# A hybrid decoder trunk on one core: one semaphore wait and three row loads moved, the LRU convolution cut in chunks, its gate products in fp32r passes

## The chip, the core and the metric

One of the cores of a Trainium2 chip runs the whole kernel. The metric is the device time of one execution in microseconds (us), as the median of several runs; lower is better. Five engines work side by side, each through its own list of instructions in the order in which it was written: TensorE (PE in the rows, its weight loads PEld), VectorE (DVE), ScalarE (ACT), GpSimd (POOL) and SyncE (SP), which here only issues DMAs. They meet through semaphores: an instruction may wait until a counter has a value, and an engine stands still while its next instruction waits.

## The reference, cut to what matters

Four layers, each `x + W_out(mixer(RMSNorm(x)) * silu(gate))`, over 1024 prompt positions and 8 sample positions, in fp32. The mixers are retention (layers 0 and 3), differential attention (layer 1) and the RG-LRU block (layer 2). What the change touches of it:

```
def retention_chunk(S0, qkv, lg):                        # layers 0, 3: 4 heads, 8 chunks of 128
    o = einsum('bihd,bhdv->bihv', q, S0) * q_dec + (q k^T * decay) v
    S = exp(C * lg) * S0 + einsum('bjhd,bjhv->bhdv', k * k_dec, v)
...
def rg_lru_branch(h, ...):                               # layer 2: 12 blocks of 128 channels
    xb, g = split(h @ w_in, 2)
    xconv = conv_b + sum(xc[:, kk:kk + T] * conv_w[kk] for kk in range(4))   # per channel, 4 taps
    r = sigmoid(einsum('btnc,ncd->btnd', xblk, wa) + ba)                     # the gate products,
    i = sigmoid(einsum('btnc,ncd->btnd', xblk, wx) + bx)                     # 128x128 per block
    a = exp(-8 * r * softplus(-lam)); b = sqrt(1 - a^2) * (i * xconv)
    hs = scan(h <- a h + b);  out = (hs * silu(g)) @ w_out
```

## The kernel before

**Tiling.** Activations lie with channels on the 128 partitions and the T = 1032 positions along a row; a row of `xT` is one tile of 128 channels. The positions are cut in `CHUNKS` of 384, 384 and 264 columns (`NC_` = 3). A *unit* is 128 output channels: for each chunk, eight 128x128 weight tiles times the chunk. Every projection keeps fp32 precision by splitting weight and input in a high and a low part of type fp32r and making three passes for each tile: high x high (L301), low input (L302), low weight (L303). A chunk of a unit is thus 24 matmuls.

**Weights.** SP loads a unit's weights (`load_w`, L240, 512 KB); ACT rounds them to the high part (`split_hi`, L248, two halves of 512 columns); POOL subtracts for the low part (`split_lo`, L257, two halves); PE takes them from there.

**Order.** Nothing is scheduled by a program: each engine's list is written out by hand, one function for each stage and engine (`ret_pe`, `lru_act`, `out_sp`, ...).

**Retention (layers 0, 3).** For each head, after its projections, PE walks eight chunks r. A step transposes (L944), then adds up the output in the bank OB: three matmuls of the scores with the values (L953 to L955) and, for r > 0, two matmuls of the queries with the state (L959); then come the products for the state update (L964, L965). DVE adds them to the state (L1159, L1160) and counts semaphore `r_su`. PE waits for `r_su` of the step before, with two other semaphores, ahead of L953.

**Output stage of layers 0 and 3.** SP (`out_sp`, L717 to L754) loads `w_out` units and, four DMAs a chunk (`stage_load`, L414), the mixer's output and gate from HBM into a buffer that holds two chunks; chunk 2 goes into the place of chunk 0 and so waits for `h_raw`. DVE multiplies them (`stage_dve`, L435), ACT and DVE split the product (L334, L341), PE multiplies, DVE adds to `xT` (`residual_dve`, L445). Six rows of `xT` (`AWAY_ROWS`) were in HBM while their space held other data. `x_reload` (L757 to L759) brings one back (128x1032, 516 KB); each row has its own semaphore in `x_back`, and the first residual of a row waits for it.

**LRU (layer 2).** Twelve blocks. A block has six chunks s on PE: s = 0 to 2 are the block's `xb`, s = 3 to 5 its `g`. ACT copies s = 0 to 2 from PSUM into `xpad` (L1964). DVE then copies the block's parameters `lp` (L2033), three small pieces (L2038 to L2040), and runs the convolution `xcv` over the whole row: tap by tap, a small instruction for the 8 sample positions and one over 1024 columns (L2045 to L2050). PE's gate products (L1931: two weights `wax` times three chunks of `xcv`, as six fp32 matmuls; twelve records in the trace) stand between s = 4 and s = 5 and wait for the whole convolution (`l_xc`). On ACT, `split_hi` of the next unit's weights, the tanh of g (`g_tanh`, L1953) and the tanh of the gates (L1981) follow; DVE multiplies by g (`g_mul`, L2060) and scans (L2085); POOL makes the product with g (L2112) once the scan is done, and SP stores it (L1872) and issues the next weight loads behind that store.

Of the kernel before, what the change touches and what calls it, by code (L numbers as in the profile page):

```python
# [145 lines left out]
def trunk(nc, A, LAYERS=4):  # L146
    ctx = ExitStack()
    with ctx:
# [64 lines left out]
        x_saved, x_back = sem("x_saved"), sems("x_back", KT)  # L213
# [224 lines left out]
        def residual_dve(dve, unit, q, j, c, final, sqb, sqn, back):  # L438
# [4 lines left out]
            if back is not None and c == 0 and j < AWAY_ROWS:  # L443
                dve.wait_ge(x_back[j], back)
# [183 lines left out]
        def ret_sp(sp, lay):  # L628
# [59 lines left out]
            head(RH - 1)  # L688
            out_sp(sp, lay, wout, U + 48, R + 48, [(FILL_AT[lay] + 1, 0), (FILL_AT[lay] + 2, KT)], ret_stage_wait,
# [175 lines left out]
        def out_dve(dve, ch, lay, U, fills, last_layer, scale, beside=None, begun=False):  # L865
# [4 lines left out]
            for x, (f, k0) in enumerate(fills):  # L870
# [10 lines left out]
                for q, (j, c) in enumerate(out_order(more or final)):  # L881
                    residual_dve(dve, unit, q, j, c, final, sqb, sqn, 16 * (lay // 3 + 1) if lay in (0, 3) and x == 0 else None)
# [36 lines left out]
        def ret_pe(pe, lay):  # L919
            f = FILL_AT[lay]  # L920
            def head(h, first):
                unit, raw, n1, n8, ntr = ret_places(lay, h)
                for s in range(36):
# [22 lines left out]
                    if 0 <= t - 1 < NBLK:  # L946
# [905 lines left out]
        tmp_s = al.take(NS)  # L1852

        l_ld, l_set, l_z = sem("l_ld"), sem("l_set"), sem("l_z")
        l_xc = sem("l_xc")
# [7 lines left out]
        CREDITS += [(x, 1) for x in (l_xc, l_tg, l_at, l_m, l_sq, l_h, l_th, l_pr)] + [(l_gt, 12)]  # L1863
# [53 lines left out]
        def lru_pe(pe):  # L1917
            def block(n, slot, pair, first=False):
                unit, n1, n2, n3, n6 = lru_at(n)
                for s in range(6):  # L1920
                    if not (first and s < NC_):
                        unit_chunk(pe, unit, s // NC_, s % NC_, LF)
                    if s == 4:
                        pe.wait_ge(l_set, 1)
                        pe.wait_ge(l_xc, done(n1.at(0)))
                        pe.wait_ge(l_wl[slot], pair * 32 + 32)
# [7 lines left out]
            block(0, 0, 0, True)  # L1934
            block(1, 1, 0)
            for i in range(1, LRU_B // 2):
                block(i * 2, 0, i)
                block(i * 2 + 1, 1, i)
# [300 lines left out]
```

## Time and profile before

| what | value |
|---|---|
| median of 3 runs | 3273.43 us (3272.81 to 3280.8) |
| the profiled execution, its own time | 3276.99 us |
| its span in the profile | 3275.2 us |
| PE busy | 3120.3 us (95%), 19978 matmuls |
| DVE, ACT, POOL busy | 1372.2 us (42%), 1267.7 us (39%), 561.9 us (17%) |
| projection passes L301, L302, L303 busy | 1633.6, 1574.7, 1574.0 us |
| gate products L1931 busy | 33.1 us (384 columns) and 12.7 us (264 columns) |
| DMA | 459.78 MB, mean 140 GB/s |

The profile's busy time of PE overlaps (matmuls are pipelined, their ends are modelled), so what PE really loses is read from the distance between starts in the timeline: two 384-column matmuls start about 0.175 us apart, and every longer distance is a wait. "[0.58 <-DVE arena L1160]" behind a row says that the engine stood idle for 0.58 us before it and that the end of DVE's L1160 released it. "x4" joins instructions of one line that follow each other.

### The profile page before, as it was taken

How to read it: one execution, taken by the hardware profiler on the slowest of the kernel's cores; microseconds unless marked ns; L12 is line 12 of the kernel's file. 1: busy time of each engine (PE TensorE's matmuls, PEld its weight loads, DVE VectorE, ACT ScalarE, POOL GpSimd, SP SyncE). 2: the span in 40 equal slices, each digit the busy share in tenths (PEclk: the TensorE clock that was granted, in tenths of full speed). 3: DMA queues.
4: the chain of work that ended last, by engine and by line, in shares of the span. 5: the costliest groups of instructions: out<-in, count | busy, mean ns of one | idle time of the engine just before them, and what ended most of it. 6: DMA issues, size and time to landing. Idle time of an engine off the chain costs nothing.

```text
span 3275.2 us, 51546 instructions
## 1 busy us (share of the span) xinstructions
PE 3120.3 (95%) x19978; PEld 2838.0 (87%) x19978; DVE 1372.2 (42%) x3480; ACT 1267.7 (39%) x2709; POOL 561.9 (17%) x432
## 2 busy tenths in 40 slices
PE   6999999998998999999979899989799999999899
PEld 4989898997997888888859899979798989899799
DVE  3241514226344444444445777763524151422631
ACT  4332423334234555455543455532433332333321
POOL 1112021111211111011101223222111211111121
PEclk8999999999999999999999999999999999999999
DMA  5848586776413444444453122232234242425742
GB/s 164 256 151 248 168 245 194 213 240 224 145 56 116 139 136 155 142 147 143 141 187 100 34 64 63 64 106 82 63 125 129 88 148 89 151 78 163 240 138 80
DMA packets 531892, 459.78 MB, mean 140 GB/s; under 512 B 25091, under 2 KB 464387, under 8 KB 531651
## 3 DMA queue, kind: packets, MB, share of 16 engines
q1 hardware_dynamic: 425570, 334.75, 32.8%
q10 hardware_dynamic: 106080, 121.74, 10.8%
q8 instruction: 160, 2.62, 0.3%
q14 instruction: 82, 0.66, 0.1%
HBM read 354.39 MB, written 169.14 MB: 160 GB/s over the span
## 4 chain that ended last, share of the span: by engine, by line
PE 79%; DVE 10%; issue 4%; ACT 4%; DMA 2%; ACTq 1%; SPq 1%; POOL 0%; DVEq 0%
PE psum L301 20%; PE psum L302 20%; PE psum L303 20%; PE psum L959 3%; PE psum L1419 2%; DVE Hl L341 2%; PE psum L1392 2%; DVE hraw L385 2%; PE psum L936 1%; DVE hraw L435 1%; PE psum L1408 1%; PE psum L1931 1%; PE psum L1462 1%; PE psum L976 1%; PE psum L1431 1%
## 5 line engine op out<-in xcount | busy, mean ns | idle before, releaser
L301 PE MATMUL psum<-Hh,Wh 128*128 128x384 f32 (+1 forms) x4896 | 1633.6, 334 | 92.9 <-DVE Hl L341 31.6
L302 PE MATMUL psum<-Hl,Wh 128*128 128x384 f32 (+1 forms) x4896 | 1574.7, 322 | 0.0
L303 PE MATMUL psum<-Hh,Wl 128*128 128x384 f32 (+1 forms) x4896 | 1574.0, 321 | 0.0
L301 PEld LDWEIGHTS psum<-Hh,Wh 128*128 128x128 f32 x4896 | 931.5, 190 | 147.7 <-issue 55.0
L257 POOL TENSOR_TENSOR Wl<-wraw,Wh 128x512 fp32r<-128x512 f32 (+1 forms) x416 | 533.3, 1303 | 2518.3 <-ACT Wh L248 2517.2
L302 PEld LDWEIGHTS psum<-Hl,Wh 128*128 128x128 f32 x4896 | 932.3, 190 | 6.2 <-issue 0.3
L303 PEld LDWEIGHTS psum<-Hh,Wl 128*128 128x128 f32 x4896 | 930.2, 190 | 0.0
L248 ACT ACTIVATE Wh<-wraw 128x512 fp32r<-128x512 f32 (+1 forms) x416 | 235.1, 615 | 267.3 <-PE psum L303 148.2
L445 DVE TENSOR_TENSOR xT<-psum,xT 128x384 f32<-128x384 f32 x168 | 86.3, 514 | 294.8 <-PE psum L303 294.1
L334 ACT ACTIVATE Hh<-hraw 128x384 fp32r<-128x384 f32 (+1 forms) x252 | 116.5, 489 | 153.8 <-DVE hraw L435 82.4
L1020 ACT ACTIVATE hraw<-psum 128x384 f32<-128x384 f32 (+1 forms) x96 | 44.0, 458 | 279.3 <-PE psum L303 279.3
L1166 DVE SCALAR_TENSOR_TENSOR arena<-arena 128x512 f32<-128x512 f32 x128 | 98.4, 820 | 106.5 <-ACT arena L1069 106.5
L1128 DVE TENSOR_TENSOR vtl<-psum,vth 128x384 fp32r<-128x384 f32 (+1 forms) x96 | 48.6, 506 | 212.0 <-ACT vth L1042 212.0
L1660 ACT ACTIVATE arena<-arena 128x256 f32<-128x256 f32 (+7 forms) x128 | 98.2, 769 | 86.7 <-DVE arena L1725 86.7
L341 DVE TENSOR_TENSOR Hl<-hraw,Hh 128x384 fp32r<-128x384 f32 (+1 forms) x252 | 119.5, 510 | 13.7 <-ACT Hh L334 13.2
L1122 DVE SCALAR_TENSOR_TENSOR ktl<-psum,arena,kth 128x384 fp32r<-128x384 f32 (+1 forms) x48 | 27.5, 573 | 216.8 <-ACT kth L1039 216.8
L1721 DVE CUSTOM_DVE_ANT_0 arena<-psum,arena 128x256 f32<-128x256 f32 (+7 forms) x128 | 91.9, 754 | 47.0 <-PE psum L1392 45.5
L1026 ACT ACTIVATE arena<-psum 128x384 f32<-128x384 f32 (+1 forms) x96 | 44.0, 458 | 166.7 <-PE psum L303 166.7
L959 PE MATMUL psum<-arena 128*128 128x512 f32 x224 | 105.2, 592 | 0.0
L600 DVE TENSOR_SCALAR arena<-arena 128x1 f32<-128x1 f32 x72 | 11.1, 154 | 208.7 <-ACT hraw L1064 208.7
L1074 ACT ACTIVATE arena<-psum,arena 128x512 f32<-128x512 f32 x64 | 44.1, 689 | 117.0 <-DVE arena L607 117.0
L456 ACT ACTIVATE arena<-xT 128x384 f32<-128x384 f32 (+1 forms) x72 | 35.4, 491 | 132.2 <-DVE xT L445 132.2
(212 smaller groups left out, 3164.7 us busy)
## 6 DMA issues: line engine op xcount, KB each, us to landing
wraw<-in_ret_w_in SPq DMA_DIRECT2D x96, 512.0 KB, 4.4
scratch_kc<-in_cache_kt SPq DMA_DIRECT2D x64, 512.0 KB, 6.4
scratch_vc<-in_cache_vt SPq DMA_DIRECT2D x64, 512.0 KB, 6.7
arena<-in_state_ret ACTq DMA_DIRECT2D x64, 512.0 KB, 6.9
out_ret_state_sample<-arena ACTq DMA_DIRECT2D x64, 512.0 KB, 5.1
arena<-scratch_kc SPq DMA_DIRECT2D x64, 512.0 KB, 4.3
arena<-scratch_vc SPq DMA_DIRECT2D x64, 512.0 KB, 4.5
scratch_on<-arena ACTq DMA_DIRECT2D x78, 256.0 KB, 2.4
```

What stands on the lines that cost most here:

```text
L248: act.activation(Wh[:, j % 2, x], wraw[:, j % 2, x], ACT.Copy).then_inc(w_hi, 1)
L257: pool.tensor_tensor(Wl[:, j % 2, x], wraw[:, j % 2, x], Wh[:, j % 2, x].bitcast(F32), ALU.subtract)\
L301: nc.tensor.matmul(out, hi, xh, start=(k == 0), stop=False)
L302: nc.tensor.matmul(out, hi, xl, start=False, stop=False)
L303: last = nc.tensor.matmul(out, lo, xh, start=False, stop=(k == kt - 1))
L334: act.activation(Hh[:, k, c0:c0 + w], hraw[:, n % HR, 0:w], ACT.Copy).then_inc(h_hi, 1)
L341: nc.vector.tensor_tensor(Hl[:, k, c0:c0 + w], hraw[:, n % HR, 0:w], Hh[:, k, c0:c0 + w].bitcast(F32), ALU.subtract).then_inc(h_lo, 1)
L445: nc.vector.tensor_tensor(xT[:, j, c0:c0 + w], bank[q % 2][:, 0:w], xT[:, j, c0:c0 + w], ALU.add)\
L959: last = nc.tensor.matmul(OB[:, :], qdT[:, r % 2, x, :], St[:, x, :], start=False, stop=(x == 1))
L1166: last = nc.vector.scalar_tensor_tensor(sring[:, b % 4, x, :], vbr[:, b % 4, :], kT[:, x, SEQ + b:SEQ + b + 1], sring[:, b % 4, x, :], ALU ...
L1660: act.activation(x, x, ACT.Exp, bias=nm2[:, s % 2, m:m + 1], accum_out=(l8[:, s:s + 1], l1[:, s % 2:s % 2 + 1])[m]).then_inc(d_ex, 1)
L1721: nc.vector.tensor_tensor_reduce(out=(S0[t % 3], S1[t % 2])[m][:, 0:W], in0=SSC[m][:, 0:W], in1=strip[:, SEQ - W:SEQ], scale=1.0, scalar=- ...
```

## The change

Four edits, all in the hand-written orders.

1. **Row reloads.** Three of the six rows of `xT` are issued at the end of the last retention head, each behind a value of `r_st`, ahead of the first `w_out` load; the others go one place earlier in `out_sp`. Rows share a semaphore in pairs, and a residual waits for both rows of its pair (32).
2. **State wait.** PE's wait for `r_su` stands behind the three score matmuls, ahead of L960.
3. **Convolution by chunk.** DVE runs the four taps chunk by chunk (`conv(0)`, `conv(1)`, `conv(2)`) and makes a low part of each chunk (`conv_low`, into `xcl`) from a high part that ACT rounds (`conv_high`, into `xch`). ACT also rounds the gate weights (`wxh`), POOL subtracts for `wxl` (`gate_lo`, between the two units' `split_lo`).
4. **Gate products.** Eighteen fp32r matmuls (three passes, two weights, three chunks) take the place of six fp32 ones, still between s = 4 and s = 5; each chunk waits for its own `l_xl`.

```
-                        pe.wait_ge(r_su, prior(n8.at(r)))
                         nc.tensor.matmul(OB[:, :], sdh[:, r % 2, :], vth[:, r, :], start=True, stop=False)
...
                         last = nc.tensor.matmul(OB[:, :], sdl[:, r % 2, :], vth[:, r, :], start=False, stop=(r == 0))
+                        pe.wait_ge(r_su, prior(n8.at(r)))
...
             head(RH - 1)
+            for k in range(3):
+                sp.wait_ge(r_st, done(8 * RH * (j_ + 1) - 8 + 2 * k + 2))
+                x_reload(sp, lay, k)
...
-                        if lay in (0, 3):
-                            x_reload(sp, lay, j)
...
-                    if lay in (0, 3) and x == 0 and j < AWAY_ROWS:
-                        x_reload(sp, lay, j)
+                    if lay in (0, 3) and x == 0 and j + 1 < AWAY_ROWS:
+                        x_reload(sp, lay, j + 1)
...
-                                nc.tensor.matmul(bank[2 + 3 * x + c][:, 0:w], wax[:, slot, x, :], xcv[:, c0:c0 + w],
-                                                 start=True, stop=True).then_inc(l_gt, 1)
+                            pe.wait_ge(l_xl, done(n3.at(c)))
...
+                                nc.tensor.matmul(out, wxh[:, x, :], xch[:, c0:c0 + w], start=True, stop=False)
+                                nc.tensor.matmul(out, wxh[:, x, :], xcl[:, c0:c0 + w], start=False, stop=False)
+                                nc.tensor.matmul(out, wxl[:, x, :], xch[:, c0:c0 + w], start=False, stop=True)\
+                                    .then_inc(l_gt, 1)
...
+                act.wait_ge(l_wl[n % 2], n // 2 * 32 + 32)
+                act.activation(wxh, wax[:, n % 2, :, :], ACT.Copy).then_inc(l_wh, 1)
...
                 split_hi(act, unit, unit, 2)
+                def conv_high(c):
+                    act.wait_ge(l_xc, done(n3.at(c)))
+                    act.activation(xch[:, c0:c0 + w], xcv[:, c0:c0 + w], ACT.Copy).then_inc(l_xh, 1)
+                conv_high(0)
+                conv_high(1)
                 g_tanh(0)
+                conv_high(2)
                 g_tanh(1)
...
+                def conv_low(c):
+                    dve.wait_ge(l_xh, done(n3.at(c)))
+                    nc.vector.tensor_tensor(xcl[:, c0:c0 + w], xcv[:, c0:c0 + w], xch[:, c0:c0 + w].bitcast(F32),
+                                            ALU.subtract).then_inc(l_xl, 1)
+                conv(0)
+                conv(1)
+                conv_low(0)
+                conv(2)
                 nc.vector.tensor_copy(lo[:, OC:OC + 3], xpad[:, SEQ:SEQ + 3])
...
+                conv_low(1)
                 g_mul(0)
+                conv_low(2)
                 g_mul(1)
```

PE, one step of the retention, r > 0, before:

```order
L944 MATMUL psum<-ident,arena 128x128 x3
L953 MATMUL psum<-vth,sdh 128x512 [waits r_su,r_on,r_sd]
L954 MATMUL psum<-vtl,sdh 128x512
L955 MATMUL psum<-vth,sdl 128x512
L959 MATMUL psum<-arena 128x512 [waits r_qd]
```

and with the change:

```order
L945 MATMUL psum<-ident,arena 128x128 x3
L953 MATMUL psum<-vth,sdh 128x512 [waits r_on,r_sd]
L954 MATMUL psum<-vtl,sdh 128x512
L955 MATMUL psum<-vth,sdl 128x512
L960 MATMUL psum<-arena 128x512 [waits r_qd,r_su]
```

Three matmuls now stand ahead of the wait for the state.

SP at the end of layer 0, from the first `w_out` load to the loads of chunk 2, before (`xT<-in_x_cols` is a row reload, `arena<-scratch_on` and `arena<-scratch_g` are the chunk loads; 128x4x264 is chunk 2):

```order
L240 DMA wraw<-in_ret_w_out 128x8x128 [waits raw_free]
L414 DMA arena<-scratch_on 128x4x384 [waits r_g_st0,r_on_st0,r_on_st1,r_qz,r_g_st1,r_qd,r_os_st,r_sn,r_st]
...
L759 DMA xT<-in_x_cols 128x1032
L240 DMA wraw<-in_ret_w_out 128x8x128 [waits raw_free]
L414 DMA arena<-scratch_on 128x4x384 [waits r_so,r_S_st,r_su,r_o]
...
L759 DMA xT<-in_x_cols 128x1032 x2
L240 DMA wraw<-in_ret_w_out 128x8x128 [waits raw_free]
L759 DMA xT<-in_x_cols 128x1032
L414 DMA arena<-scratch_on 128x4x264 [waits h_raw]
```

and with the change:

```order
L760 DMA xT<-in_x_cols 128x1032 [waits r_st] x3
L240 DMA wraw<-in_ret_w_out 128x8x128 [waits raw_free]
L414 DMA arena<-scratch_on 128x4x384 [waits r_g_st0,r_on_st0,r_on_st1,r_qz,r_g_st1,r_qd,r_os_st,r_sn,r_st]
...
L240 DMA wraw<-in_ret_w_out 128x8x128 [waits raw_free]
L414 DMA arena<-scratch_on 128x4x384 [waits r_so,r_S_st,r_su,r_o]
...
L760 DMA xT<-in_x_cols 128x1032
L240 DMA wraw<-in_ret_w_out 128x8x128 [waits raw_free]
L760 DMA xT<-in_x_cols 128x1032
L414 DMA arena<-scratch_on 128x4x264 [waits h_raw]
```

Between the first load of chunk 0 and that of chunk 2 there were four row reloads, and there are two.

DVE in one LRU block, before (L2046 and L2050 are the taps, L2060 is `g_mul`):

```order
L2033 COPY arena<-arena 128x41 [waits dve_own]
L2038 COPY arena<-arena 128x3 [waits l_gt,unit_ev,dve_own]
...
L2046 TENSOR_SCALAR arena<-arena 128x1024
...
L2050 SCALAR_TENSOR_TENSOR arena<-arena 128x1024
...
L2050 SCALAR_TENSOR_TENSOR arena<-arena 128x1024
L2060 SCALAR_TENSOR_TENSOR arena<-arena,psum 128x384 [waits unit_ev,l_th] x2
```

and with the change (L2069 and L2072 are the taps, L2081 is `conv_low`, L2097 is `g_mul`):

```order
L2050 COPY arena<-arena 128x41 [waits dve_own]
L2069 TENSOR_SCALAR arena<-arena 128x384 [waits unit_ev,l_gt,dve_own]
L2072 SCALAR_TENSOR_TENSOR arena<-arena 128x384 [waits dve_own] x3
L2069 TENSOR_SCALAR arena<-arena 128x384 [waits unit_ev]
L2072 SCALAR_TENSOR_TENSOR arena<-arena 128x384 [waits dve_own] x3
L2081 TENSOR_TENSOR xcl<-arena,xch 128x384 [waits l_xh]
L2065 TENSOR_SCALAR arena<-arena 128x8 [waits unit_ev]
...
L2072 SCALAR_TENSOR_TENSOR arena<-arena 128x256
L2088 COPY arena<-arena 128x3
...
L2081 TENSOR_TENSOR xcl<-arena,xch 128x384 [waits l_xh]
L2097 SCALAR_TENSOR_TENSOR arena<-arena,psum 128x384 [waits unit_ev,l_th]
```

The first low part, which waits for ACT, now stands ahead of the last chunk's taps.

ACT in the same block, before (L1964 copies into `xpad`, L248 rounds the next unit's weights, L1953 is `g_tanh`, L1981 the gates):

```order
L1964 ACTIVATE arena<-psum 128x256
L248 ACTIVATE Wh<-wraw 128x512 [waits unit_ps,w_loaded0]
L248 ACTIVATE Wh<-wraw 128x512
L1953 ACT_TABLE_LOAD [waits l_pr]
L1953 ACTIVATE arena<-psum 128x384 [waits unit_ps]
L1953 ACTIVATE arena<-psum 128x384 [waits l_pr,unit_ps]
L1981 ACTIVATE arena<-psum,arena 128x384 [waits l_gt] x4
```

and with the change (L1978 is `conv_high`):

```order
L1972 ACTIVATE arena<-psum 128x256
L248 ACTIVATE Wh<-wraw 128x512 [waits unit_ps,w_loaded0]
L248 ACTIVATE Wh<-wraw 128x512
L1978 ACTIVATE xch<-arena 128x384 [waits l_xc] x2
L1959 ACT_TABLE_LOAD [waits l_pr]
L1959 ACTIVATE arena<-psum 128x384 [waits unit_ps]
L1978 ACTIVATE xch<-arena 128x264 [waits l_xc]
L1959 ACTIVATE arena<-psum 128x384 [waits l_pr,unit_ps]
L1998 ACTIVATE arena<-psum,arena 128x384 [waits l_gt] x4
```

Both high parts that PE needs first stand behind a wait for the weight load `w_loaded0`.

## Rows read from the trace of the kernel before

**Rows 1.** Page, busy time, share and instructions of each engine.

```profile
PE 3120.3 (95%) x19978; PEld 2838.0 (87%) x19978; DVE 1372.2 (42%) x3480; ACT 1267.7 (39%) x2709; POOL 561.9 (17%) x432
```

**Rows 2.** PE timeline, two retention steps: start, us, engine, line, operation [idle <-releaser].

```profile
191.76 0.60 PE L944 MATMUL psum<-ident,arena 128*128 128x128 f32 x4
192.95 0.47 PE L953 MATMUL psum<-vth,sdh 128*128 128x512 f32 x1 [0.58 <-DVE arena L1160]
...
193.73 1.02 PE L959 MATMUL psum<-arena 128*128 128x512 f32 x2
...
201.50 0.60 PE L944 MATMUL psum<-ident,arena 128*128 128x128 f32 x4
201.86 0.48 PE L953 MATMUL psum<-vth,sdh 128*128 128x512 f32 x1
```

**Rows 3.** What PE's L953 waited for in the whole span: us, times.

```profile
  DVE arena L1160: 13.2, 24
```

**Rows 4.** PE timeline, first matmul of chunk 2 in layers 0 and 3.

```profile
818.00 0.39 PE L301 MATMUL psum<-Hh,Wh 128*128 128x264 f32 x1 [2.73 <-DVE xT L445]
...
3106.11 0.39 PE L301 MATMUL psum<-Hh,Wh 128*128 128x264 f32 x1 [2.82 <-DVE xT L445]
```

**Rows 5.** SP timeline, layer 0: fourth reload, first load of chunk 2.

```profile
798.76 5.04 SPq L759 DMA_DIRECT2D xT<-in_x_cols  x1
803.84 0.43 SPq L414 DMA_DIRECT2D arena<-scratch_on  x1
```

**Rows 6.** DVE timeline, layer 0: first products of chunk 2.

```profile
814.51 1.12 DVE L435 SCALAR_TENSOR_TENSOR hraw<-arena 128x264 f32<-128x264 f32 x3 [3.94 <-DMA arena<-scratch_g]
```

**Rows 7.** Windows: each engine's busy us, granted clock, DMA share, GB/s.

```profile
736.00:746.00 10.00, 9.73 (x59) 8.12 (x57) 5.14 (x19) 4.09 (x8) 0.00 (x0) 1.00 0.15 47
...
816.00:826.00 10.00, 7.88 (x58) 7.67 (x59) 6.10 (x16) 4.36 (x10) 3.21 (x3) 1.00 1.08 365
...
3106.90:3110.30 3.40, 3.40 (x18) 3.40 (x17) 2.46 (x7) 1.06 (x3) 0.00 (x0) 0.51 1.06 375
```

**Rows 8.** PE timeline, gate products of an LRU block; the last row, the next block's.

```profile
1959.22 0.34 PE L303 MATMUL psum<-Hh,Wl 128*128 128x384 f32 x1
1959.40 3.64 PE L1931 MATMUL psum<-arena 128*128 128x384 f32 x12
1962.68 0.48 PE L301 MATMUL psum<-Hh,Wh 128*128 128x264 f32 x1
1963.00 0.28 PE L302 MATMUL psum<-Hl,Wh 128*128 128x264 f32 x1
...
1986.08 0.81 PE L1931 MATMUL psum<-arena 128*128 128x384 f32 x2
```

**Rows 9.** DVE timeline, the same block: parameters, second tap, fourth tap.

```profile
1949.64 1.21 DVE L2033 COPY arena<-arena 128x41 f32<-128x41 f32 x1
...
1953.31 1.28 DVE L2050 SCALAR_TENSOR_TENSOR arena<-arena 128x1024 f32<-128x1024 f32 x1
...
1956.23 2.38 DVE L2050 SCALAR_TENSOR_TENSOR arena<-arena 128x1024 f32<-128x1024 f32 x1
```

**Rows 10.** ACT timeline, the same block.

```profile
1955.52 1.15 ACT L248 ACTIVATE Wh<-wraw 128x512 fp32r<-128x512 f32 x2 [4.08 <-DMA wraw<-in_lru_w_in]
1956.69 1.28 ACT L1953 ACT_TABLE_LOAD   x1
```

**Rows 11.** POOL timeline, the same block: low parts of two units.

```profile
1949.52 2.52 POOL L257 TENSOR_TENSOR Wl<-wraw,Wh 128x512 fp32r<-128x512 f32 x2
1956.23 3.52 POOL L257 TENSOR_TENSOR Wl<-wraw,Wh 128x512 fp32r<-128x512 f32 x2 [4.19 <-ACT Wh L248]
```

**Rows 12.** ACT's waits in 1844 to 2160: us, times, longest.

```profile
ACT Wh L248 <- DMA wraw<-in_lru_w_in: 40.9, 10, 4.4
```

**Rows 13.** PE timeline, last LRU block: gates, then chunk s = 5.

```profile
2154.61 0.55 PE L301 MATMUL psum<-Hh,Wh 128*128 128x264 f32 x1 [4.36 <-DVE arena L2060]
```

**Rows 14.** ACT timeline, last LRU block.

```profile
2150.93 1.15 ACT L248 ACTIVATE Wh<-wraw 128x512 fp32r<-128x512 f32 x2 [12.27 <-DMA wraw<-in_lru_w_out]
```

More of the change, by code:

```diff
@@ L881, in out_dve @@
                 for q, (j, c) in enumerate(out_order(more or final)):
-                    residual_dve(dve, unit, q, j, c, final, sqb, sqn, 16 * (lay // 3 + 1) if lay in (0, 3) and x == 0 else None)
+                    residual_dve(dve, unit, q, j, c, final, sqb, sqn, 32 * (lay // 3 + 1) if lay in (0, 3) and x == 0 else None)
                     sqn += final
@@ L1862, in trunk @@
         l_oev = sem("l_oev")
-        CREDITS += [(x, 1) for x in (l_xc, l_tg, l_at, l_m, l_sq, l_h, l_th, l_pr)] + [(l_gt, 12)]
+        CREDITS += [(x, 1) for x in (l_xc, l_xh, l_xl, l_wh, l_wlo, l_tg, l_at, l_m, l_sq, l_h, l_th, l_pr)] + [(l_gt, 12)]
         CREDITS += [(x, 16) for x in (l_hst,)]
@@ L1917, in lru_pe, with block @@
         def lru_pe(pe):
-            def block(n, slot, pair, first=False):
+            def block(n, first=False):
                 unit, n1, n2, n3, n6 = lru_at(n)
@@ L1924, in block @@
                         pe.wait_ge(l_set, 1)
-                        pe.wait_ge(l_xc, done(n1.at(0)))
-                        pe.wait_ge(l_wl[slot], pair * 32 + 32)
+                        pe.wait_ge(l_wlo, done(n1.at(0)))
                         pe.wait_ge(l_tg, prior(n6.at(0)))
@@ L1929, in block @@
                             c0, w = CHUNKS[c]
+                            pe.wait_ge(l_xl, done(n3.at(c)))
                             for x in range(2):
-                                nc.tensor.matmul(bank[2 + 3 * x + c][:, 0:w], wax[:, slot, x, :], xcv[:, c0:c0 + w],
-                                                 start=True, stop=True).then_inc(l_gt, 1)
[L1934 to L1938, printed above, removed]
+                                out = bank[2 + 3 * x + c][:, 0:w]
+                                nc.tensor.matmul(out, wxh[:, x, :], xch[:, c0:c0 + w], start=True, stop=False)
+                                nc.tensor.matmul(out, wxh[:, x, :], xcl[:, c0:c0 + w], start=False, stop=False)
+                                nc.tensor.matmul(out, wxl[:, x, :], xch[:, c0:c0 + w], start=False, stop=True)\
+                                    .then_inc(l_gt, 1)
+            block(0, True)
+            for n in range(1, LRU_B):
+                block(n)
             out_pe(pe, 2, LU + LRU_IN, [(6, 0), (7, KT)], LAST == 2)
@@ L2037, in block, with conv @@
                 oc = lo[:, OCS:OCS + 24].rearrange("p (b r) -> p b r", r=3)
+                def conv(c):
+                    c0, w = CHUNKS[c]
+                    dve.wait_ge(unit_ev, ev_val(unit.at(0), c))
+                    wp = min(w, SEQ - c0)
+                    for k in range(4):
+                        tap = lp[:, LW + k:LW + k + 1]
+                        src = xpad[:, c0 + k:c0 + k + wp]
+                        if wp < w:
+                            src_s = cs[:, :, k] if k < 3 else xs8
+                            if k == 0:
+                                nc.vector.tensor_scalar(xcv[:, SEQ:T], src_s, tap, lp[:, LB:LB + 1], ALU.mult, ALU.add)
+                            else:
+                                nc.vector.scalar_tensor_tensor(xcv[:, SEQ:T], src_s, tap, xcv[:, SEQ:T], ALU.mult, ALU.add)
+                        if k == 0:
+                            ins = nc.vector.tensor_scalar(xcv[:, c0:c0 + wp], src, tap, lp[:, LB:LB + 1], ALU.mult,
+                                                          ALU.add)
+                        else:
+                            ins = nc.vector.scalar_tensor_tensor(xcv[:, c0:c0 + wp], src, tap, xcv[:, c0:c0 + wp],
+                                                                 ALU.mult, ALU.add)
+                        if k < 3:
+                            ch.link(ins)
+                    ins.then_inc(l_xc, 1)
+                def conv_low(c):
+                    c0, w = CHUNKS[c]
+                    dve.wait_ge(l_xh, done(n3.at(c)))
[5 more added lines that the diff above has]
+                conv(2)
                 nc.vector.tensor_copy(lo[:, OC:OC + 3], xpad[:, SEQ:SEQ + 3])
@@ L2103, in lru_pool, with gate_lo @@
         def lru_pool(pool):
+            def gate_lo(n):
+                pool.wait_ge(l_wh, done(n))
+                pool.tensor_tensor(wxl, wax[:, n % 2, :, :], wxh.bitcast(F32), ALU.subtract).then_inc(l_wlo, 1)
             def block(n, js):
@@ L2106, in block @@
                     split_lo(pool, Pos(LU, n, 2), j + 1)
+                    if j == js[0]:
+                        gate_lo(n)
                 product(n)
@@ L2118, in lru_pool @@
                 split_lo(pool, Pos(LU, LRU_B - 1, 2), j + 1)
+                if j == 0:
+                    gate_lo(LRU_B - 1)
             out_pool(pool, 2, LU + LRU_IN, [(6, 0), (7, KT)], LAST == 2, beside={3: lambda: product(LRU_B - 1)})
```

30 lines of the change are left out of this document (10 added, 20 removed).

## The prediction

> **What bounds the kernel now.** I read the busy table first: PE is busy for 3120.3 of 3275.2 us, the other engines for less than half [rows 1]. So only what changes the distance between starts on PE can move the time, and I looked at PE's timeline at the four places that the change touches: the retention steps, where PE stands idle ahead of L953 until DVE's state update ends [rows 2]; the output stage of layers 0 and 3, where chunk 2 starts late [rows 4]; the gate products of an LRU block, with no idle time ahead of them [rows 8]; and the end of the last LRU block [rows 13]. Then I followed the engine that PE waits for, or will wait for, at each place: SP and DVE in the output stage [rows 5, 6], DVE, ACT and POOL in the LRU block [rows 9 to 12].
>
> The sum is made against the profiled execution, 3276.99 us, which lies 3.56 above the median of the runs, 3273.43; I take that off at the end. About 0.3% (9.8 us) is what a measurement of this kernel can tell from no change, so "faster" is below 3263.6 and "slower" above 3283.3.
>
> **The state wait.** In a stalled step L953 starts 1.19 us after L944, in a free one 0.36 us after it [rows 2]: 0.83 lost. With the wait behind three matmuls, which take 0.78 (192.95 to 193.73 [rows 2]), L953 starts at 192.12, the three are through at 192.90, and the state comes at the same moment as before, so that L960 starts at about 192.95 where L959 started at 193.73: 0.78 won. What triggers DVE's update is PE's own work of the step before, so the chain moves along with PE and the gain stays in each step. There are 24 such waits, 13.2 us of idle time, 0.55 each [rows 3]. That idle time is the low bound of the gain, 24 x 0.78 = 18.7 the high one; I take 24 x 0.69 = 16.5, the middle and a little, since the weight load of L960 can now lie behind the wait as well. **-16.5 (-13.2 to -18.7).** Nothing else is queued behind this wait but PE itself.
>
> **The row loads.** Chunk 2 starts after 2.73 us of idle time in layer 0, 2.82 in layer 3 [rows 4]. The releaser shown is a residual, but that residual stood on DVE behind the products of chunk 2, and these waited 3.94 us for a load that landed at about 814.5 [rows 6], although SP issued the first of them at 803.84 [rows 5]. The reload just ahead of it took 5.04 us to issue, the load itself 0.43 [rows 5]: the queue was full. At 365 GB/s, with a DMA share of 1.08 [rows 7], one row (516 KB, 0.528 MB) takes 1.45 us. Two rows fewer ahead of chunk 2 make it 2.9 us earlier, against 2.73 and 2.82 needed: just enough. If both gaps close that is -5.5, and the half-speed stretch behind the second goes too: 3.40 us at a granted 0.51, the 1.2 GHz level [rows 7], half of which is 1.7. Together -7.2; what DVE still has to do ahead of the residual can keep a part. The three rows now go out during the last head, where the DMA share is 0.15 (736 to 746 [rows 7]), so they cost nothing there; the first w_out load now stands behind them on SP, behind the value of r_st for r = 6, and if it came late, PE would lose that time one for one. **-6 (-7.2 to 0).** Joining two rows to one semaphore makes a residual wait for its neighbour's row too; both are issued long before, so 0.
>
> **The gate products alone.** Now they take 1959.40 to 1962.68, 3.28 us [rows 8]. A 384-column pass starts 0.18 us after the one before (1959.22 to 1959.40 [rows 8]), a 264-column one by its columns 0.12. Twelve and six of them: 12 x 0.175 + 6 x 0.12 = 2.8. The first matmul behind the fp32 products also took 0.32 instead of 0.12 (1962.68 to 1963.00 [rows 8]). Saved: 0.46 to 0.66 a block, if no operand is late.
>
> **Their operands.** PE wants chunk 0 at 1959.40 and chunk 1 at 1959.40 + 6 x 0.175 = 1960.45. I put the new instructions in the time of that block.
>
> ACT: it waits 4.08 us for the weight load, then rounds until 1956.67 [rows 10]; ten blocks wait so, 40.9 us in all [rows 12]. Both high parts are queued behind this. At 0.5 us each (1.15 for two of 512 columns [rows 10]) they end at 1957.2 and 1957.7.
>
> DVE: one tap over 1024 columns takes 1.28 [rows 9], three products of 264 columns 1.12 [rows 6]; for 384 columns that is 0.5, so conv(0) and conv(1) take 2.1 each, conv(2) 2.3 with its small sample taps, a low part 0.54, the three copies about 0.5. The parameters are there at 1950.85 [rows 9].
>
> POOL: two halves take 2.52 when alone [rows 11], the new gate_lo (256 columns) about 0.7. DVE and POOL hold each other up: the fourth tap took 2.38 where the second took 1.28 [rows 9], just while POOL's pair took 3.52 instead of 2.52 [rows 11], and a copy of 41 elements took 1.21 beside POOL's first half of the other pair [rows 9, 11].
>
> Put together: POOL's second half and gate_lo run until about 1952.8 against conv(0); conv(1) ends at about 1956.7. From there DVE has conv_low(0), conv(2), the copies and conv_low(1) before chunk 1 can go: 0.54 + 2.3 + 0.5 + 0.54 = 3.9. With no hindrance, and from 1957.2 when the first high part is there, it ends at 1961.1; PE then waits 0.65. With every half of POOL in the way, in both pairs, it ends at about 1963.35; PE waits 2.9. I take 1962.25, a wait of 1.8, nearer to the second, since the rows show the taking of turns in this very place. Net for a block: -0.46 + 1.8 = +1.35, bounds 0.65 - 0.66 = 0 and 2.9 - 0.46 = +2.45. What hid the convolution until now was PE's chunk s = 4; that cover ends at 1959.40. Blocks 1 to 10: **+13.5 (0 to +24.5).** Block 0 has no such load to wait for: -0.3.
>
> [...]
>
> **The last block.** ACT waits 12.27 us for the w_out load, until 2150.93 [rows 14]; the gates ran during that wait, and PE then stood 4.36 us until g_mul at 2154.61 [rows 13]. Now the gates stand behind the high parts, which stand behind that wait: 2150.93 + 1.15 + 0.5 = 2152.6 for conv_high(0), then DVE's 3.9 gives 2156.5, or 2159.0 with POOL's pair (2.52), then PE's chunks 1 and 2 (1.05 + 0.72): s = 5 at 2158.3 to 2160.8, 3.7 to 6.2 later than 2154.61. **+5.**
>
> **The clock.** After 2.82 us of idle time the granted clock fell to 0.51, after 2.73 it stayed at 1.00 (816 to 826) [rows 4, 7]. A wait of 1.8 lies below both, but comes in each block; I put in +1, for less than one such stretch of 1.7.
>
> Sum: 3276.99 - 16.5 - 6 + 13.5 - 0.3 + 5 + 1 = 3273.7; less 3.56: **3270 us**, no change that can be told.
>
> **The rivals.** (a) *Faster, about 3257.* DVE gets through the conv in time, because POOL's halves fall in its idle moments: the wait is 0.65, LRU blocks give 0. Then 3270 - 13.5 = 3256.5. For it: DVE is idle most of the time [rows 1]. Against it: the place is just where POOL and DVE meet [rows 9, 11]. Chance 0.22. (b) *Slower, about 3289.* DVE's work in line costs PE 2.9 us ahead of gate chunk 1 in blocks 1 to 10, and that is past the 2.82 at which the clock was seen to fall: +11 on the forecast, and 1.7 in half of the blocks is +8.5 more: 3289; in all of them 3297. It decides at an idle time of between 2.73 and 2.82 us. For it: 0.51 after 2.82 [rows 4, 7]; against: 1.00 after 2.73, and the wait may be shorter. Chance 0.15. (c) *The state wait only moves.* Another semaphore ahead of L960, or its weights, keeps PE for the same time: 3270 + 16.5 = 3286. Against it: in the stalled step only the state was late [rows 2]. Chance 0.05. (d) *The row loads do not do what they are for.* Chunk 2 is late because the queue is full with or without the two rows: 3270 + 6 = 3276. The 1.45 us for a row leave only 0.1 to spare, so this can be; chance 0.08.
>
> **How the numbers follow.** My forecast, 3262 to 3280 by itself, has 0.5. Faster by over 0.3%: (a) and 0.06 of the forecast's low end, 0.28. Slower: (b), (c) and a little of the forecast, 0.2. Within 0.3%: 0.52. The range from 3256 to 3288 takes in (a), (c), (d) and the low part of (b).
>
> **What would show it.** L953 without idle time and L960 with under 0.15: the state wait is right. Chunk 2 of the output stages without its 2.7 us: the row loads. In an LRU block, a period between gate products of about 28.0 where it was 26.68 (1959.40 to 1986.08 [rows 8]), with an idle time of 1.8 released by the second conv_low in the middle of the gates: the operands. A period at or below 26.7 gives (a); one above 29, with a clock near 0.5 behind the gates, (b). The forecast is wrong if the retention steps show no gain, or if PE waits in a place that I have not named.

## The result, and the profile after

| | before | changed |
|---|---|---|
| median | 3275.03 us (20 runs) | 3280.06 us (20 runs, 3274.18 to 3286.57) |
| ratio to before | | 1.0014, 95% interval 1.0008 to 1.0021 |
| profiled execution, span | 3275.2 us | 3274.0 us |

By the ratio the change makes the kernel 4.6 us slower (0.14%); the prediction had said 3270, some 3 to 5 us faster than before. The time is inside the range of what was called "no change", but the sign is wrong. The profiled execution of the changed kernel is one of its fastest: its span lies some 4 us under that of its median run. So its parts are read from it, and their sum from the medians. The state wait, the row loads and the gate products by themselves behaved nearly as forecast; the LRU layer as a whole cost more than the first two gave.

**The state wait.** PE timeline after, the step of [rows 2], and behind it what the weight loads of L960 (PEld) waited for in the whole span (us, times, longest):

```profile
188.12 0.60 PE L945 MATMUL psum<-ident,arena 128*128 128x128 f32 x4
188.48 0.48 PE L953 MATMUL psum<-vth,sdh 128*128 128x512 f32 x1
...
189.27 1.06 PE L960 MATMUL psum<-arena 128*128 128x512 f32 x2
```

```profile
PEld psum L960 <- DVE arena L1161: 3.8, 17, 0.4
```

L953 follows L944 (now L945) after 0.36 us, as in a free step, and L960 starts 1.15 us after L945 where L959 had started 1.97 us after L944. The 13.2 us of idle time [rows 3] are gone: no matmul of L960 stands idle for over 0.15 us anywhere in the span. The 3.8 us are idle time of the weight loads, which overlap the matmuls.

**The row loads.** PE timeline after, the two places of [rows 4]:

```profile
804.39 0.39 PE L301 MATMUL psum<-Hh,Wh 128*128 128x264 f32 x1 [0.93 <-DVE xT L445]
```

```profile
3106.05 0.39 PE L301 MATMUL psum<-Hh,Wh 128*128 128x264 f32 x1 [0.85 <-DVE xT L445]
```

2.73 and 2.82 have become 0.93 and 0.85.

**The LRU layer.** What PE waited for in the LRU blocks (1840 to 2180: us, times, longest; ten of the fourteen waits stand ahead of gate chunk 1 in the blocks 1 to 10), and the PE timeline of one block's gates (1949.15), of another's (2010.84):

```profile
PE psum L1937 <- DVE xcl L2081: 28.5, 14, 7.5
```

```profile
1948.68 0.34 PE L303 MATMUL psum<-Hh,Wl 128*128 128x384 f32 x1
1949.15 0.41 PE L1937 MATMUL psum<-xch,wxh 128*128 128x384 f32 x1
...
1950.11 0.33 PE L1939 MATMUL psum<-xch,wxl 128*128 128x384 f32 x1
1952.24 0.45 PE L1937 MATMUL psum<-xch,wxh 128*128 128x384 f32 x1 [1.80 <-DVE xcl L2081]
1952.52 0.33 PE L1938 MATMUL psum<-xcl,wxh 128*128 128x384 f32 x1
```

```profile
2010.84 0.45 PE L1937 MATMUL psum<-xch,wxh 128*128 128x384 f32 x1 [1.80 <-DVE xcl L2081]
...
2012.00 0.42 PE L1937 MATMUL psum<-xch,wxh 128*128 128x264 f32 x1
2012.22 0.42 PE L1938 MATMUL psum<-xcl,wxh 128*128 128x264 f32 x1
```

The wait is there, in its place, and 1.80 us long. In the second block the passes over 264 columns then start 0.22 us apart, where they normally take 0.12: the clock has fallen. The windows after say which blocks: each engine's busy us, the granted clock (third number from the end), DMA share, GB/s.

```profile
1947.00:1975.00 28.00, 25.80 (x160) 24.74 (x159) 23.47 (x37) 14.15 (x25) 7.22 (x6) 1.00 0.21 62
...
2005.00:2034.00 29.00, 27.09 (x161) 26.48 (x161) 24.00 (x37) 15.21 (x27) 8.40 (x7) 0.94 0.20 60
```

Four of the ten blocks that wait read 0.94, the other six 1.00. A mean of 0.94 over 29 us is 3.5 us at half speed, which by itself would lose about 1.7 us (an estimate). A block at full clock has a period of 28.34 (1949.15 to the next block's gates at 1977.49) where [rows 8] have 26.68.

Why the wait is 1.80 is seen on DVE, ACT and POOL in the same block (L2128 and L2050 are the copies, L2069 and L2072 the taps, L2081 `conv_low`):

```profile
1936.82 2.24 DVE L2128 COPY arena<-arena 128x36 f32<-128x36 f32 x1
1939.09 1.22 DVE L2050 COPY arena<-arena 128x41 f32<-128x41 f32 x1
1940.35 1.38 DVE L2069 TENSOR_SCALAR arena<-arena 128x384 f32<-128x384 f32 x1
1941.76 2.38 DVE L2072 SCALAR_TENSOR_TENSOR arena<-arena 128x384 f32<-128x384 f32 x3
1944.06 0.47 DVE L2069 TENSOR_SCALAR arena<-arena 128x384 f32<-128x384 f32 x1
1944.57 2.87 DVE L2072 SCALAR_TENSOR_TENSOR arena<-arena 128x384 f32<-128x384 f32 x3
1947.36 1.64 DVE L2081 TENSOR_TENSOR xcl<-arena,xch 128x384 fp32r<-128x384 f32 x1
...
1951.63 0.55 DVE L2081 TENSOR_TENSOR xcl<-arena,xch 128x384 fp32r<-128x384 f32 x1
```

```profile
1945.02 1.15 ACT L248 ACTIVATE Wh<-wraw 128x512 fp32r<-128x512 f32 x2 [4.15 <-DMA wraw<-in_lru_w_in]
1946.08 0.51 ACT L1978 ACTIVATE xch<-arena 128x384 fp32r<-128x384 f32 x1
```

```profile
1936.60 2.42 POOL L2156 TENSOR_TENSOR arena<-arena 128x1032 f32<-128x1032 f32 x1 [16.65 <-DVE arena L2123]
1938.98 2.53 POOL L257 TENSOR_TENSOR Wl<-wraw,Wh 128x512 fp32r<-128x512 f32 x2
1941.69 0.73 POOL L2144 TENSOR_TENSOR wxl<-arena,wxh 128x256 fp32r<-128x256 f32 x1 [0.18 <-POOL Wl L257]
1945.73 2.85 POOL L257 TENSOR_TENSOR Wl<-wraw,Wh 128x512 fp32r<-128x512 f32 x2 [3.31 <-ACT Wh L248]
```

Read DVE's column against POOL's: wherever POOL works, one DVE instruction is about as much longer as POOL needs for one of its own. The first tap takes 1.38 against 0.47 for the same tap of chunk 1, a low part 1.64 against 0.55. ACT does not hold DVE up in this block, nor in seven others of the ten; in the remaining two DVE waits 0.77 and 0.85 us for the first high part, and there PE's idle time is 2.24 and 2.30 us instead of 1.65 to 1.81.

**The last block.** PE timeline and ACT timeline after; [rows 13, 14] answer to them.

```profile
2151.44 0.34 PE L303 MATMUL psum<-Hh,Wl 128*128 128x384 f32 x1
2159.26 0.66 PE L1937 MATMUL psum<-xch,wxh 128*128 128x384 f32 x1 [7.48 <-DVE xcl L2081]
...
2163.32 0.69 PE L1937 MATMUL psum<-xch,wxh 128*128 128x384 f32 x1 [1.80 <-DVE xcl L2081]
...
2166.72 0.42 PE L301 MATMUL psum<-Hh,Wh 128*128 128x264 f32 x1
```

```profile
2156.72 1.15 ACT L248 ACTIVATE Wh<-wraw 128x512 fp32r<-128x512 f32 x2 [13.06 <-DMA wraw<-in_lru_w_out]
```

Before, the gates ran while ACT waited for the w_out load. Now they wait for it too, and run at half clock behind it.

### The profile page after: what moved, and what is told of

It is laid out like the page before. It is cut to its first block, busy times and chain, and to the rows that moved or that the text cites. A ratio compares the mean times of both kernels' runs of the same rounds, so it can differ in the third digit from the quotient of the medians.

```text
span 3274.0 us, 51934 instructions
## 1 busy us (share of the span) xinstructions
PE 3119.6 (95%) x20050; PEld 2850.4 (87%) x20050; DVE 1428.3 (44%) x3612; ACT 1281.3 (39%) x2757; POOL 567.2 (17%) x444
## 4 chain that ended last, share of the span: by engine, by line
PE 77%; DVE 13%; ACT 3%; issue 3%; DMA 2%; SPq 1%; POOL 0%; ACTq 0%; DVEq 0%
PE psum L301 19%; PE psum L302 19%; PE psum L303 19%; PE psum L960 3%; PE psum L1393 2%; PE psum L1420 2%; DVE Hl L341 2%; DVE hraw L385 2%; DVE arena L2072 2%; PE psum L937 1%; PE psum L1409 1%; DVE hraw L435 1%; PE psum L1463 1%; PE psum L1432 1%; PE psum L986 1%
## 5 line engine op out<-in xcount | busy, mean ns | idle before, releaser
L248 ACT ACTIVATE Wh<-wraw 128x512 fp32r<-128x512 f32 (+1 forms) x416 | 235.1, 615 | 266.0 <-PE psum L303 141.1
L960 PE MATMUL psum<-arena 128*128 128x512 f32 x224 | 106.0, 596 | 0.0
```

Of the source, the lines that this page charges most:

```text
L248: act.activation(Wh[:, j % 2, x], wraw[:, j % 2, x], ACT.Copy).then_inc(w_hi, 1)
L960: last = nc.tensor.matmul(OB[:, :], qdT[:, r % 2, x, :], St[:, x, :], start=False, stop=(x == 1))
```

## The experiments

Each ratio is against the kernel before, run on the same chip; "idle" is the commonest idle time ahead of gate chunk 1 in the LRU blocks 1 to 10, "period" that of a block at full clock, and the last number says in how many of these ten blocks the granted clock reads 0.94.

| kernel | median us | ratio | 95% interval | idle us, period us, blocks at 0.94 |
|---|---|---|---|---|
| state wait alone | 3260.05 | 0.9955 | 0.9941 to 0.9968 | |
| row loads alone | 3270.35 | 0.9982 | 0.9973 to 0.9991 | |
| both, LRU as before | 3254.36 | 0.9933 | 0.9920 to 0.9947 | |
| changed kernel | 3280.06 | 1.0014 | 1.0008 to 1.0021 | 1.80, 28.4, 4 of 10 |
| changed, wait filled | 3274.17 | 1.0001 | 0.9992 to 1.0010 | (filled), 28.6, 0 |
| changed, high parts first | 3272.67 | 0.9994 | 0.9985 to 1.0003 | 2.13, 28.6, 4 of 10 |
| changed, no copies | 3268.74 | 0.9978 | 0.9969 to 0.9987 | 1.35, 27.9, 2 of 10 |
| both of these | 3262.08 | 0.9958 | 0.9944 to 0.9971 | 1.26, 27.8, 0 |
| and late split in the last block | 3252.64 | 0.9931 | 0.9918 to 0.9945 | 1.26, 27.8, 0 |
| changed, POOL later | 3263.13 | 0.9960 | 0.9946 to 0.9973 | 0.2 to 0.5, 27.3, 1 of 10 |
| all edits | 3237.48 | 0.9882 | 0.9867 to 0.9897 | none, 26.3, 0 |
| both, LRU as before, late split | 3248.05 | 0.9915 | 0.9901 to 0.9929 | |

### The two retention edits, alone and together

The diffs are the first two parts of the change; the first kernel takes only the `r_su` lines, the second only the `x_reload` lines with their semaphores, the third both.

> The kernel before with the state wait alone moved behind the three score matmuls. Theory (each of 24 stalled steps gains about 0.74 us, as the traces of before and after show it between the same matmuls): 17.7 us less than before, ratio 0.9946, no idle time ahead of L953, and under 0.15 us ahead of the state matmuls. Rival (another wait takes its place, or the gain is eaten later in the head): under 10 us less, ratio above 0.997.

> The kernel before with the row reloads alone moved. Theory: the late start of chunk 2 in the output stages of layers 0 and 3 closes from 2.73 and 2.82 us of idle time to about 0.9 each, and the half-speed stretch behind the second one goes: 4 to 6 us less than before, ratio 0.9982 to 0.9988. Rival (the chunk loads are bound by the full queue or by DVE with or without the two rows; what differs between the two traces there is chance): within 1.5 us of before.

> The kernel before with the state wait and the row reloads moved, the LRU layer as before. Theory (the parts add up, and the LRU edits cost some 28 us, about 16 of it a steady 1.6 us in each of ten blocks, 5 to 6 in the last block, the rest half-speed stretches): 22 to 23 us less than before, ratio 0.993; the changed kernel stands 27 to 28 us above this one. Rival (the LRU edits cost only the 18 us that were forecast, and the rest of the miss is a smaller gain of the other two): 13 us less than before, ratio 0.996.

Measured: 0.9955, 0.9982 and 0.9933, that is 14.7, 5.9 and 21.9 us less than before. The parts add up (20.6 by their sum). The first is 3 us below its theory, which its interval takes in (0.9941 to 0.9968); ahead of the state matmuls two waits of 0.36 and 0.35 us are left, where under 0.15 was expected (us, times, longest):

```profile
PE psum L959 <- DVE arena L1160: 0.7, 2, 0.4
```

In the second the gaps ahead of chunk 2 shrank to 0.51 us and to less than 0.15, further than the 0.9 that was expected. The third lies at the edge of its theory and far from its rival.

What the LRU edits cost follows: 1.0014 less 0.9933 is 0.81%, 26.5 us (some 5 either way by the two intervals), not the 19 that were forecast (13.5 - 0.3 + 5 + 1).

### The wait filled with spare matmuls

```
+                            if c == 1:
+                                for _ in range(10):
+                                    nc.tensor.matmul(bank[3][:, 0:CHUNKS[0][1]], wxh[:, 0, :],
+                                                     xch[:, 0:CHUNKS[0][1]], start=True, stop=True)
                             pe.wait_ge(l_xl, done(n3.at(c)))
```

> The changed kernel with ten spare matmuls of 384 columns on PE between gate chunk 0 and the wait for chunk 1 in each LRU block (1.75 us of work in a wait of 1.8, written to a bank that the next product overwrites). It splits the price of the wait from that of the clock. Theory (the recurring 1.8 us wait lets the clock fall in four or more of ten blocks, 1.7 us each): the period of a block stays at about 28.4, no block shows a granted clock under 1.00, and the time falls 7 to 12 us below the changed kernel, to 0.998 of before. Rival (the half-speed stretches come from elsewhere, or fall where PE waits anyway): the time stays within 2 us of the changed kernel, 1.0014 of before.

Measured 1.0001 against 1.0014: 4.3 us less by the ratios, 5.9 by the medians. PE runs through (the ten spare matmuls, then chunk 1), and the window of a block that read 0.94 before reads 1.00, as do all ten:

```profile
1981.41 1.91 PE L1936 MATMUL psum<-xch,wxh 128*128 128x384 f32 x10
1983.37 0.44 PE L1940 MATMUL psum<-xch,wxh 128*128 128x384 f32 x1
```

```profile
2005.00:2034.00 29.00, 28.56 (x176) 27.49 (x175) 24.47 (x37) 14.79 (x27) 8.61 (x6) 1.00 0.21 63
```

So doing useless work for as long as the wait lasts makes the kernel faster, by 4 to 6 us where 7 to 12 were expected, while the wait itself, 1.96 us a block between starts, stays. The spare matmuls also stand in block 0, where nothing waits, and cost 1.74 us there (a period of 28.18 instead of 26.44), so the clock's own price is that much higher. By the times alone the rival (within 2 us) is not out, since the intervals of the two kernels just touch (0.9992 to 1.0010, 1.0008 to 1.0021); what speaks against it is the clock, full in all ten blocks.

### A two by two on what makes the second low part late

```
-                split_hi(act, unit, unit, 2)
...
                 conv_high(0)
                 conv_high(1)
+                split_hi(act, unit, unit, 2)
                 g_tanh(0)
```

> The changed kernel with ACT's conv_high(0) and conv_high(1) ahead of the split of the next unit's weights, so that they no longer stand behind the wait for the weight load. One half of a two by two with the next kernels: what makes conv_low(1) late, ACT's wait for the weights (theory A) or DVE's own work, held up by POOL, from the end of the scan on (theory B)? A: the 0.85 us that DVE waits for the first high part go, the idle time ahead of gate chunk 1 falls from 1.8 to about 0.9, no block shows a granted clock under 1.00, and the last block wins 4.5 since its high parts no longer wait for the w_out load: 18 less than the changed kernel, 3262, ratio 0.996. B: the idle time stays at 1.5 or more and only the last block wins: 3275, ratio 1.000.

```
-                ch.link(nc.vector.tensor_copy(lp, lpar[:, bass.ds(n, 1), :].rearrange("p a c -> p (a c)")))
+                lp, lo = lpar[:, n, :], lout[:, n, :]
...
-                ch.link(nc.vector.tensor_copy(lout[:, bass.ds(n, 1), :].rearrange("p a c -> p (a c)"), lo))
```

> The changed kernel without two copies on DVE in each LRU block (parameters into lp, results out of lo: both are addressed in place), which took 1.22 and 2.24 us because POOL held them up, 0.2 each otherwise. A (ACT's wait binds): DVE comes to conv_low(0) more than 1 us earlier and waits there for the high part; the idle time ahead of gate chunk 1 stays at 1.4 or more; within 4 us of the changed kernel, ratio 1.000 to 1.0014. B (DVE's work with POOL binds): idle time under 0.7, ratio 0.996.

> Both edits of the two kernels before it. If A and B each cover a part (my reading: the two run side by side and each alone hides the other's gain), the idle time ahead of gate chunk 1 is 0.2 or less, the period of an LRU block 26.2 to 26.4 where the kernel before has 26.7, the clock 1.00 in all blocks, and the time 3248 to 3251, ratio 0.992, a little under the kernel with the state wait and the row reloads alone (0.9933). Rival: POOL's second pair still stands in the way of conv(2); idle 0.5 or more, ratio 0.994.

Theory A fell. With the high parts first, DVE does not wait for ACT any more, yet the idle time ahead of chunk 1 grew (PE timeline of one block):

```profile
1982.05 0.34 PE L303 MATMUL psum<-Hh,Wl 128*128 128x384 f32 x1
1982.22 0.34 PE L1937 MATMUL psum<-xch,wxh 128*128 128x384 f32 x1
...
1985.56 0.44 PE L1937 MATMUL psum<-xch,wxh 128*128 128x384 f32 x1 [2.12 <-DVE xcl L2081]
```

Nine blocks last as long as in the changed kernel (260.1 against 260.5 us for the nine periods together). Of the 6.5 to 7.4 us that were won, 4.1 lie in the last block by the two traces (from the gates before it to chunk s = 5: 39.37 instead of 43.43); the rest was not located, and the profiled execution, 3277.38 us, is the slowest of the eleven. The DVE and POOL timelines of the same block show why nothing was won in the nine blocks: conv(2) meets both halves of POOL's pair.

```profile
1977.94 1.93 DVE L2072 SCALAR_TENSOR_TENSOR arena<-arena 128x384 f32<-128x384 f32 x3
1979.78 0.55 DVE L2081 TENSOR_TENSOR xcl<-arena,xch 128x384 fp32r<-128x384 f32 x1
...
1981.03 1.57 DVE L2072 SCALAR_TENSOR_TENSOR arena<-arena 128x256 f32<-128x256 f32 x1
1982.64 1.13 DVE L2067 SCALAR_TENSOR_TENSOR arena<-arena 128x8 f32<-128x8 f32 x1
1983.69 0.47 DVE L2072 SCALAR_TENSOR_TENSOR arena<-arena 128x256 f32<-128x256 f32 x1
```

```profile
1981.02 2.72 POOL L257 TENSOR_TENSOR Wl<-wraw,Wh 128x512 fp32r<-128x512 f32 x2 [5.24 <-ACT Wh L248]
```

A sample tap over 8 columns takes 1.13 instead of 0.23, a tap over 256 columns 1.57 instead of 0.48: 2.0 us held. In the changed kernel DVE lost as much in each block, at other instructions: in eight of the ten the pair held conv(1) and the first low part (2.87 against 1.93, 1.64 against 0.55); in the other two DVE waited 0.77 and 0.85 us for ACT, and the pair held the first low part and a sample tap (0.82 against 0.55, 1.25 against 0.28). From the first tap to the end of the second low part DVE takes 11.8 us in this block as in that at 1949.15. The idle time grew because chunk 0 of the gates no longer starts late: 0.17 us behind the pass before it, where it was 0.47.

The kernel without copies came between the two theories: idle time mostly 1.34 to 1.51, 0.9978, 11 us less than the changed kernel by the medians where A gave 4 at most and B 17 or so. Both edits together left 1.26 where I expected 0.2, and 0.9958, above even the rival's 0.994; the rival named there (POOL's pair ahead of conv(2)) is what remained:

```profile
1978.24 0.45 PE L1937 MATMUL psum<-xch,wxh 128*128 128x384 f32 x1 [1.26 <-DVE xcl L2082]
```

None of the ten blocks of that kernel lost its clock.

### POOL's pair out of the way

```
                 for j in js:
+                    if len(js) == 2 and j == 1:
+                        pool.wait_ge(l_xl, done(Pos(0, n, 3).at(1)))
                     split_lo(pool, Pos(LU, n, 2), j + 1)
```

> The changed kernel with one wait more, on POOL: its second pair of low weight parts in a block (2.5 us, for the next block) starts once conv_low(1) is done. A test of the step that stayed after the two by two, where the idle time ahead of gate chunk 1 went only from 1.8 to 1.26: that POOL's pair, run beside conv(2), holds DVE up. Theory: the tap of 1.56, the sample tap of 1.14 or 1.25 and the low part of 0.82 fall back to 0.48, 0.23 and 0.55; conv_low(1) ends 1.3 to 1.5 us earlier, PE waits 0.3 to 0.5 there, all granted clocks are 1.00, and the time falls by 15 + 5: 3260, ratio 0.9955. Rival (POOL's pair does not matter, or is now late for the next unit): idle 1.5 or more there, or a new idle time of over 1 us ahead of chunk s = 0; ratio 1.000 or above.

Measured 0.9960, 17 us less than the changed kernel, from one wait on an engine that is busy for 17% of the span. The DVE timeline:

```profile
1971.38 1.93 DVE L2072 SCALAR_TENSOR_TENSOR arena<-arena 128x384 f32<-128x384 f32 x3
1974.22 0.56 DVE L2081 TENSOR_TENSOR xcl<-arena,xch 128x384 fp32r<-128x384 f32 x1 [0.91 <-ACT xch L1978]
...
1975.48 0.48 DVE L2072 SCALAR_TENSOR_TENSOR arena<-arena 128x256 f32<-128x256 f32 x1
...
1978.35 1.28 DVE L2081 TENSOR_TENSOR xcl<-arena,xch 128x264 fp32r<-128x264 f32 x1
```

The taps of conv(1) take 1.93 where they took 2.87, the first low part 0.56 where it took 1.64, and conv(2) is not held either (0.48 a tap); POOL's first half now meets the third low part (1.28), and PE waits twice in most blocks, 0.2 to 0.5 us ahead of chunk 1 and ahead of chunk 2. In two blocks it waited 1.16 and 1.25 us at the first of the two places instead, and behind the 1.16 the clock fell, where no fall at all was expected. The last block, which this wait does not touch, still costs what it did.

### All edits, and the old LRU with the same care

The late split in the last block, here on top of "both of these"; the kernel with all edits has POOL's wait besides, the one with the old LRU the same two `split_hi` lines around its own `g_tanh` calls:

```
+                if not last:
+                    split_hi(act, unit, unit, 2)
                 g_tanh(0)
                 conv_high(2)
                 g_tanh(1)
                 if last:
+                    split_hi(act, unit, unit, 2)
```

> The kernel before it with, in the last LRU block alone, the split of the first w_out unit behind the high parts and the tanh of g. Theory: chunk s = 5 no longer waits for the w_out load (4.36 us of idle time in the kernel before), and the split is not needed earlier: 3 to 4 us less, 3245 to 3247, ratio 0.991. Rival: the w_out split, which DVE and PE wait for behind it, comes later by as much, and the time stays within 1 us.

The late split won 9 us, not 3 to 4: I had set it against the 4.36 of [rows 13], but in the kernel it was added to, the third high part still stood behind the w_out load, and gate chunk 2 waited 6.71 us:

```profile
2151.64 0.59 PE L1937 MATMUL psum<-xch,wxh 128*128 128x264 f32 x1 [6.71 <-DVE xcl L2082]
```

> The kernel with the high parts first, without the two copies and with the late split in the last block, and with POOL's wait besides. Theory: no idle time over 0.3 us in the middle of the gates, a period of 26.2 to 26.4 for an LRU block, ten times 1.5 less than without POOL's wait: 3237 to 3240, ratio 0.989, 14 us under the kernel with the state wait and the row reloads alone. Rival (the loop from the gates over ACT, the scan and the convolution back to the gates is then bound by something else): period 27.3 or more, 3248, ratio 0.992.

> The state wait and the row reloads with the LRU layer as before, but the last block's split of the w_out unit behind the tanh of g, as in the kernel before it: what is the best that the old gate products give? Theory: the 4.36 us ahead of chunk s = 5 go, and with them a half-speed stretch of 1.7: 3249 to 3250, ratio 0.992; the kernel with all edits then stands 10 to 12 us below it, which is the worth of fp32r gates once nothing waits for them and of the freed loop. Rival: the two are within 3 us, so the fp32r gates are worth nothing even then.

All edits together: 3237.48, 1.2% under before and in the expected span. The gates run through (PE timeline, chunk 0 to the first pass of s = 5):

```profile
1969.58 0.34 PE L1937 MATMUL psum<-xch,wxh 128*128 128x384 f32 x1
...
1972.55 0.28 PE L301 MATMUL psum<-Hh,Wh 128*128 128x264 f32 x1
```

2.97 us, where [rows 8] have 3.28 and a slow first pass behind it. The old gate products with the late split give 3248.05, 10.6 us more. The block periods of the two (26.29 and 26.73, eleven of them) explain 5 us of that; where the rest lies was not followed up.

## Why the prediction was wrong, point by point

The step that failed is the price of the LRU edits, 19 us in the sum and 26.5 in the runs: the wait ahead of gate chunk 1 came as said, but it was priced by its idle time, the clock term was set at +1 by a threshold that does not hold, and the last block was put too low. The retention edits gave what was forecast (21.9 us against 22.5), so these 7 us turned the sign.

- **The state wait: right.** -16.5 with bounds of -13.2 and -18.7; alone it measured -14.7. The traces give 0.75 for each of the 24 steps, 18.0, from the first stalled step of a layer to its last in both kernels.
- **The row loads: right.** -6, measured -5.9. The two gaps did not close, which was the forecast at its best, but shrank by 1.8 and 2.0, and the half-speed stretch behind the second is gone.
- **The gate products alone: right.** The first block, which waits for nothing, has a period of 26.44 against 26.70, -0.26 where -0.3 was forecast.
- **Their operands: the wait right, its price low.** Forecast 1.8, measured 1.80 in most blocks, released by the second `conv_low` as said. But 1.8 is idle time, and PE pays by starts: 1950.11 to 1952.24 is 2.13 instead of 0.175, so 1.96. Chunk 0 of the next block's xb besides starts 0.14 later than before (0.61 behind the pass ahead of it instead of 0.47), since `g_mul` comes late. Net +1.66 a block instead of +1.35: 3 us over ten blocks. That 1.8 itself was met is partly luck: it is all but the middle of the two bounds, 0.65 and 2.9, and the forecast let DVE wait for the first high part, which it does in two of the ten blocks only.
- **The clock: wrong.** I read a threshold out of two rows, 1.00 after 2.73 and 0.51 after 2.82 [rows 4, 7], found 1.8 safely below it and put in +1. The clock fell in four blocks of the profiled execution, two of them behind just 1.80. The four periods behind a fall are 0.8 to 1.9 longer than 28.34, 4.8 together, and filling the wait is worth 4 to 6 us. Two single rows are no threshold; rival (b) had the right mechanism and the wrong point from which it decides.
- **The last block: right in kind, short by 2.** Chunk s = 5 starts 15.1 us after the gates could (2151.6 to 2166.72) instead of 8.0 (2146.60 to 2154.61): +7.1 instead of +5. Chunks 1 and 2 of the gates ran at half clock behind the long wait (2163.32 to 2166.72, 3.4 instead of the 1.77 of the forecast), and the w_out load came 0.8 later against PE (5.1 behind the moment at which the gates could start, where it was 4.3).
- **The sum.** With 3 + 4 + 2 more, the LRU part is 28 instead of 19, as the traces have it (from the first gates to s = 5 of the last block 330.3 us instead of 302.5); the 26.5 of the runs agree within their intervals. Besides, 3273.43, on which the 3270 stands, was the median of three runs; twenty gave 3275.03, so 1.6 of the miss in the time (not in the sign) is there.

The Trainium skill (SBUF — State Buffer, "Who interferes with whom") states that a VectorE instruction with two SBUF inputs contends with a GpSimd instruction that reads SBUF, and that copies and tensor_scalar instructions can contend with GpSimd too, in their two-port modes. The traces agree: beside POOL's pair, taps and low parts with two inputs took 1.57, 1.13 and 1.64 against 0.48, 0.23 and 0.55, and of those with one input the 41-column copy took 1.22 against 0.18 in block 0 and the first tap 1.38 against 0.47. The run with POOL's wait, which keeps the second pair away from the convolution, is 17 us faster. Which mode an instruction ran in, no run here shows.

## What to carry to other kernels

The changed kernel is slower because a loop that had 0.8 us to spare (the convolution ended at 1956.23 + 2.38 [rows 9], the gates began at 1959.40 [rows 8]: gates on PE, their tanh on ACT, states and scan and convolution on DVE, back to the gates) was lengthened by more than PE's saving. Before work is split among engines, follow such a loop once around with the holds that engines put on each other, and look for an engine of low use whose work can be moved out of its way by a wait: here one wait on POOL was worth 17 us. A wait of PE that recurs should be priced by the distance between starts (0.16 more than the idle time here) and with a chance of the clock falling, not by its idle time alone.

## What was not expected of the hardware

- The granted clock fell to half in four of ten blocks with idle times of 1.80, 1.80, 2.24 and 2.30, and stayed full in the others, with 1.65 to 1.81. With the high parts first nine of ten idle times were 2.12 to 2.15; the clock fell behind four of these and stayed behind five. With 1.26 in each of the ten blocks it fell in none, but in the kernel with POOL's wait it fell behind 1.16. So the length of one wait does not decide, and what does was not settled.
- DVE and POOL held each other at the grain of instructions: an 8-column tap of 0.23 took 1.13 and a 36-column copy 2.24, about as long as the POOL instruction beside it (1.36, half of the pair's 2.72, and 2.42).
